# Hybrid layer: three-pass projections between the steps of the delta rule, convolution by pairs of chunks, modulation columns made in three places

## What is computed

```python
mod = cond @ mod_w[layer] + mod_b[layer]             # cond = silu(c)
sh1, sc1, g1, sh2, sc2, g2 = jnp.split(mod, 6)       # 6 x 1024
h = rmsnorm(x, norm_mix) * (1 + sc1) + sh1
qkv_a, z_a, b_a, a_a, q_b, k_b, v_b = split(h @ w_in)   # 1536, 512, 4, 4, 3 x 512
qkv_a = silu(causal_conv(qkv_a, 4 taps))             # then l2norm of q_a, k_a
o_a = rmsnorm(gated_delta_rule(q_a, k_a, v_a, g, beta)) * silu(z_a)
o_b = attention(rope(q_b), rope(k_b), v_b)           # 4 heads of 128
x = x + g1 * (concat(o_a, o_b) @ w_out)
x = x + g2 * peer_ffn(rmsnorm(x) * (1 + sc2) + sh2)  # 16384 experts, top 16
```

## Time and profile before

| | |
|---|---|
| median of 3 runs | 3955.04 us |
| the profiled execution's own time | 3955.51 us |
| its span (first to last instruction) | 3953.7 us |
| mean granted TensorE clock | 0.941 |
| TensorE busy | 3589.6 us (91%) |
| VectorE busy | 1980.6 us (50%) |
| ScalarE busy | 1753.2 us (44%) |
| DMA queue 1 | 562 MB, 43.1% of 16 engines |
| hybrid layer, start to its last product | 0 to 456.5 us |

### The profile page before, as it was taken

One profiled execution on the slowest core, in us unless ns is written; L12 is line 12 of the kernel. 1 busy time (PEld: TensorE's weight loads), 2 busy tenths in 40 slices (PEclk: granted clock), 3 DMA queues, 4 the chain that ended last, 5 costly groups with the idle time before them and its releaser, 6 DMA issues.

```text
span 3953.7 us, 54864 instructions
## 1 busy us (share of the span) xinstructions
PE 3589.6 (91%) x22798; PEld 3178.6 (80%) x22798; DVE 1980.6 (50%) x3117; ACT 1753.2 (44%) x2671; POOL 639.0 (16%) x260
## 2 busy tenths in 40 slices
PE   7777799999999889999999997979879989898799
PEld 4456699998888757999988885869879967688699
DVE  0321267565776331956655555564444446644443
ACT  1321145665444321556654543544545335345453
POOL 0000068664000000886620000000000000000000
PEclk9887899999999979999999997989899989899999
DMA  5421245445887422454456553223424623133245
GB/s 200 149 85 48 80 140 181 145 140 173 277 278 234 154 75 101 155 173 142 140 182 194 194 173 121 87 93 118 160 97 143 171 80 110 64 139 129 106 150 139
DMA packets 265628, 565.50 MB, mean 143 GB/s; under 512 B 14943, under 2 KB 91043, under 8 KB 264611
## 3 DMA queue, kind: packets, MB, share of 16 engines
q1 hardware_dynamic: 265380, 561.99, 43.1%
HBM read 560.89 MB, written 1.05 MB: 142 GB/s over the span
## 4 chain that ended last, share of the span: by engine, by line
PE 78%; DVE 6%; ACT 5%; issue 3%; DMA 2%; POOL 1%; DVEq 0%; ACTq 0%; SPq 0%
PE ps L359 7%; PE ps L361 7%; PE ps L360 7%; PE ps L286 7%; PE ps L1518 6%; PE ps L1438 6%; PE ps L1519 6%; PE ps L1439 6%; PE ps L1520 6%; PE ps L1440 6%; PE ps L1485 3%; POOL uvr_split L1809 1%; DVE ring_split L430 1%; PE ps L2122 1%; PE ps L1957 1%
## 5 line engine op out<-in xcount | busy, mean ns | idle before, releaser
L1809 POOL TENSOR_TENSOR uvr_split<-uvr,high_split 128x1024 fp32r<-128x1024 f32 x172 | 434.4, 2529 | 1301.6 <-ACT high_split L1561 1301.6
L1440 PE MATMUL ps<-consts_sb_split,uvr_split 128*128 128x256 f32 x2048 | 579.1, 283 | 0.0
L1561 ACT ACTIVATE high_split<-uvr 128x1024 fp32r<-128x1024 f32 x342 | 360.9, 1056 | 242.1 <-PE ps L1520 200.0
L361 PE MATMUL ps<-uvr_split,ring_split 128*128 128x256 f32 (+1 forms) x1584 | 454.2, 287 | 0.0
L473 ACT ACTIVATE big<-ps 128x512 f32<-128x512 f32 (+1 forms) x232 | 136.1, 586 | 627.9 <-PE ps L286 227.0
L1438 PE MATMUL ps<-consts_sb_split,high_split 128*128 128x256 f32 x1376 | 397.6, 289 | 2.9 <-ACT big L473 1.8
L1519 PE MATMUL ps<-uvr_split,hot_split 128*128 128x512 f32 x1024 | 399.1, 390 | 0.0
L1440 PEld LDWEIGHTS ps<-consts_sb_split,uvr_split 128*128 128x128 f32 x2048 | 392.0, 191 | 0.0
L1439 PE MATMUL ps<-ht_split,high_split 128*128 128x256 f32 x1376 | 389.0, 283 | 0.0
L430 DVE TENSOR_TENSOR ring_split<-big,hot_split 128x2048 fp32r<-128x2048 f32 x87 | 196.8, 2262 | 261.0 <-ACT hot_split L422 260.6
L430 DVE TENSOR_TENSOR ring_split<-big,high_split 128x2048 fp32r<-128x2048 f32 (+1 forms) x87 | 196.8, 2262 | 260.8 <-ACT high_split L422 260.3
(11 more groups left out here) (394 smaller groups left out, 8471.0 us busy)
## 6 DMA issues: line engine op xcount, KB each, us to landing
uvr<-peer_uv SPq DMA_DIRECT2D x512, 512.0 KB, 3.8
big<-mlp_w SPq DMA_DIRECT2D x32, 2048.0 KB, 8.9
big<-w_in SPq DMA_DIRECT2D x26, 2048.0 KB, 7.8
big<-mod_w SPq DMA_DIRECT2D x12, 2048.0 KB, 8.1
uvr<-mod_w SPq DMA_DIRECT2D x48, 512.0 KB, 6.6
big<-peer_w_q SPq DMA_DIRECT2D x8, 2048.0 KB, 7.9
big<-hy_w_in SPq DMA_DIRECT2D x7, 2048.0 KB, 8.7
big<-w_out SPq DMA_DIRECT2D x4, 2048.0 KB, 7.8
```

The lines of the kernel that those rows point to most:

```text
L361: m = mm(out, wl, x_high[:, k, :], start=False, stop=en)
L1440: return mm(out, w_low, x_high, start=False, stop=stop, **kw)
L1561: SE.activation(expert_high(e), expert(e), ACT.Copy).then_inc(S["expert_high"], 1)
L1809: GE.tensor_tensor(expert_low(j), expert(j), expert_high(j).bitcast(F32), ALU.subtract)\
```

## The change

- The projections of the layer become three-pass (`hybrid_linears`, a generator of 15 pieces: q/k 4, b/a 1, v 2, z 2, attention q, k, v 2 each). `hybrid_pe` runs seven at once, and the others one at a time: after the gate rows, after k.q, in each of the 5 rounds between the squaring and the inverse product, and the last behind u and w. The output projection (4 pieces) is three-pass too. The input is split in place after the block norm.
- `split_high` and `split_low` of these pieces are put between the other work of `hybrid_act` and `hybrid_dve`. The convolution runs pair by pair as the pieces come: ScalarE evicts a pair and writes the fourth tap with a scaled copy, VectorE adds three taps (36 instructions in all), ScalarE then does Silu and Square of the pair.
- Modulation tiles 0 to 3 are made on VectorE before the block norm (`mod_early_dve`: 8 scaled sums of 128x512 for each tile, then 4 small matmuls). Tiles 4 to 7 are made on TensorE behind the four chunk steps, 8 and 9 between the first heads of the attention. Tiles 10 and 11 (g2) become a seventh segment in expert layer 0.
- Rope angles and rotations move into the rounds and ahead of the chunk steps; attention follows the delta rule at once.
- `roots_act` does all Ln first, then one Exp, for every caller (the second model has callers with 6 and 4 groups; the delta rule 8 and 4).
- SP issues the vectors first, then the first modulation tile, then the other five inputs. The squares of the block norm no longer wait for the modulation.
- N (`kk_out`) is made ahead of the scaled k; the scratch places are laid out anew.

```diff
         def plan_hybrid():
-            plan_cols("gdn_qkv", w, 0, 1536)
+            plan_cols("gdn_qk", w, 0, 1024)
+            plan("gdn_ba", ...)
+            plan_cols("gdn_v", w, 1024, 1536)
             plan_cols("gdn_z", w, 1536, 2048)
-            plan("gdn_ba", ...)
-            plan_mod(0, 4, 12)
             plan_cols("moba_q", w, 2056, 2568)
             plan_cols("moba_k", w, 2568, 3080)
             plan_cols("moba_v", w, 3080, 3592)
+            plan_mod(0, 4, 10)
             plan_cols("hy_out", a["hy_w_out"][0], 0, D)

         def roots_act(rs, ngroups, mean):
...
                 SE.activation(rs[:, g0:g0 + n, :], t..., ACT.Ln, scale=1.0 / mean, bias=eps_col)
-                SE.activation(rs[:, g0:g0 + n, :], rs[:, g0:g0 + n, :], ACT.Exp, scale=-0.5)
+            SE.activation(rs[:, 0:ngroups, :], rs[:, 0:ngroups, :], ACT.Exp, scale=-0.5)

+        def mod_early_dve():
...
+            for i in range(EARLY):
+                VE.wait_ge(S[f"weights_in_{i % RING}"], weights_in(i))
+                for k in range(DC):
...
+                        VE.scalar_tensor_tensor(out=mod_total[i % 2], in0=w[:, k, :],
+                            scalar=condv[:, k:k + 1], in1=mod_total[i % 2], op0=ALU.mult, op1=ALU.add)
+                if i >= 1:
+                    columns(i - 1)

         def hybrid_pe():
             block_norm_pe(z.sq)
-            fm_linear("gdn_qkv", ...); fm_linear("gdn_z", ...); tm_linear("gdn_ba", ...)
-            mod_pe(0, 4, 8)
+            mod_early_pe()
+            linear(7)
             norm_pe([[c] for c in range(8)], 8, C["ones"], z.sq)
...
+            linear()
             TE.wait_ge(S["qk_normed"], S.nth(TE, "qk_normed"))
...
-            mod_pe(0, 8, 12)
+            linear()
             TE.wait_ge(S["n_ready"], S.nth(TE, "n_ready"))
...
-                TE.wait_ge(S["powers"], expected["powers"])
+                squared = expected["powers"]
+                linear()
+                TE.wait_ge(S["powers"], squared)
                 TE.wait_ge(S["inverse"], S.nth(TE, "inverse"))
...
+            rotate_pe("att_in", z.aq, 4, C["rot128"])
+            rotate_pe("att_in", z.ak, 4, C["rot128"])
...
+            for _ in run:
+                pass
             for c in range(NCH):
...
+                mod_unit_pe(4 + c)
             norm_pe([[c] for c in range(4)], 4, C["ones"], z.sq)
-            TE.wait_ge(S["delta_through"], S.nth(TE, "delta_through"))
-            fm_linear("moba_q", ...); fm_linear("moba_k", ...); tm_linear("moba_v", ...)
-            rotate_pe(...); rotate_pe(...)
...
+            attention_pe(4, scores, values, z.p, z.pt, between)      # mod 8, 9 at heads 0, 1
+            split_linear("hy_out", z.h_high, h_low, DC, D, "dve", "residual_in", first="x_split")

         # ScalarE, for each pair of q/k/v chunks
+            def qkv_in(i):
+                SE.activation(z.pad[:, 2 * i:2 * i + 2, 4:260], t, ACT.Copy)
+                for u in range(2):
+                    SE.activation(z.conv[:, 2 * i + u, :], t[:, u, :], ACT.Copy, scale=w[:, 2 * i + u, 3:4])
+            def silu_pair(i):
+                SE.wait_ge(S["conv_done"], S.nth(SE, "conv_done"))
...
         # expert layer 0
-        NMOD = 6 * DC
+        NMOD = 7 * DC
```

More of the change, by code:

```diff
@@ L554, in residual_dve, with gated_bank @@
             for b in range(nbanks):
[L555 to L564, removed]
-            x_complete(name)
+                gated_bank(b, gate)
+            x_complete(name)
+        def gated_bank(b, gate):
+            t = take("dve")
+            for u in range(2):
+                c = 2 * b + u
+                last = "residual_in" if u else "dve_step"
+                VE.scalar_tensor_tensor(out=x[:, c, :], in0=t[:, u * T:(u + 1) * T], scalar=gate[:, c:c + 1],
+                    in1=x[:, c, :], op0=ALU.mult, op1=ALU.add).then_inc(S[last], 1)
+                VE.wait_ge(S[last], S.nth(VE, last))
         def residual_bank(b):
@@ L1069, in hybrid_act @@
+            silu_pair(0)
+            for i in range(2, 4):
+                qkv_in(i)
+                split_high()
+                silu_pair(i - 1)
+            split_high()
+            silu_pair(3)
             SE.wait_ge(S["ba_ready"], S.nth(SE, "ba_ready"))
@@ L1075, in hybrid_act @@
             SE.wait_ge(S["ba_ln"], S.nth(SE, "ba_ln"))
+            for i in range(4, 6):
+                qkv_in(i)
+                split_high()
+            for i in range(4, 6):
+                silu_pair(i)
+            roots_act(z.rs, 8, 1.0)
+            evict_act(pairs(z.z)[0:1], ACT.Silu, frees="projections")
+            split_high()
             SE.wait_ge(S["decay_rows"], S.nth(SE, "decay_rows"))
@@ L1117, in hybrid_dve @@
+            split_low()
+            split_x_dve(h, h_low, z.h_high)
+            split_low()
             w = V["gdn_conv"].rearrange("p (c j) -> p c j", j=4)
[L1118 to L1126 removed]
@@ L1133, in hybrid_dve @@
+            for i in range(2):
+                split_low()
+                conv_pair(i)
+            split_low()
+            conv_pair(2)
+            split_low()
+            conv_pair(3)
+            VE.tensor_copy(z.ba, take("dve")[:, 0:16].rearrange("p (m n) -> p m n", m=TM)).then_inc(S["ba_out"], 1)
+            VE.wait_ge(S["ba_out"], S.nth(VE, "ba_out"))
             VE.tensor_copy(z.bb[:, :, 0:4], z.ba[:, :, 0:4]).then_inc(S["dve_step"], 1)
@@ L1775, in peer_sp @@
             uv = a["peer_uv"][L].rearrange("j p n -> p j n")
-            mod = a["mod_w"][1].rearrange("(c p) n -> p c n", p=P)
+            mod = [a["mod_w"][k].rearrange("(c p) n -> p c n", p=P) for k in range(2)]
             SP.wait_ge(S["expert_ring_free"], S.nth(SP, "expert_ring_free"))
```

406 lines of the change are left out of this document (250 added, 156 removed).

## The result

| | before | after |
|---|---|---|
| median (lowest to highest), us | 3954.3 (3948.6 to 3955.4), 4 runs | 3817.8 (3816.3 to 3821.3), 4 runs |
| profiled span, granted clock | 3953.7, 0.941 | 3816.5, 0.949 |

The ratio is 0.9657, with a 95% interval of 0.9642 to 0.9673: faster by 136.5 us. Forecast were 3818 and a range of 3788 to 3872. The sum came out to a fraction of a us.

The account below looks back on a forecast made before the run. TensorE, holding 78% of the chain's 3953.7 us, was taken as the bound. From 3955.5, minus 124.5 for the hybrid layer, plus 1.9 for g2's segment, minus 15.2 for the roots, came 3818 us; range 3788 to 3872.

Parts of the forecast that it names:

- Part 1: Start of the hybrid layer: first full-rate three-pass product near 52 us, a gain of 13 us.
- Part 2: Seven projection pieces run at once: six at 5.9 us and b/a at 5, ending near 92 us.
- Part 3: Gates to the first squaring: serial stretch with 6 us added for low clock, first squaring at 136 us against 240.5.
- Part 4: Five rounds of the inverse: 12.35 us four times and 9.7, total 59; with rotations, u and w, end at 208.5.
- Part 5: Chunk steps with modulation units, 58 us (bounds 52 and 67), ending at 266.5; then gate norm, ending at 277.
- Part 6: Attention 32 us, ending at 309; output 23 us against 29.4, ending the layer at 332 against 456.5.
- part 7: Outside the layer: +1.9 us for g2's segment, -15.2 us for fewer table loads and Exp in two layers.
- C: Rival on norms: the new Ln and Exp order spares no load, second model gives 2 us, 3831 us; chance 0.02.
- A: Rival on chunk steps: the clock stays low, 99 us for four steps instead of 58, 3859 us; chance 0.13.
- B: Rival on weight splits: they come late, exposing 4.8 us at each of twelve pieces, 3876 us; chance 0.11.
- D: Rival on TensorE: 1.2 GHz throughout the layer, added work doubles, +179 us, 3997 us; chance 0.03.
- E: Rival on the whole: nothing gained, TensorE's hours return as waits for peer weights or experts; chance 0.02.

Follow-up runs that it names:

- The run with halves: Each modulation tile of the chunk steps in two halves, eight products ahead of the wait for v, added to the run that it builds on: 3801.9 us, ratio 0.9615.
- the run that it builds on: Changed kernel with modulation tile 4 between the k.k and k.q products and the output's splits in the late order: 3807.0 us, ratio 0.9627.
- the kernel with the pairs back: Changed kernel with every norm again taking Ln and Exp pair by pair: 3853.7 us, ratio 0.9749.
- the two runs on the order: Changed kernel with Ln and Exp pair by pair again, 3853.7 us; kernel before with only all Ln first and one Exp, 3920.5 us.
- the run with the units in front: Changed kernel with modulation tiles 4 to 7 in one block ahead of the first chunk step: 3826.9 us, ratio 0.9677.
- the load order: Changed kernel with x loaded behind the second modulation tile and the constants behind the third: 3823.0 us, ratio 0.9660.
- the unit in the hole: Changed kernel with modulation tile 4 between the k.k and k.q products, the others moved up one place: 3812.5 us, ratio 0.9641.
- the late splits: Output input's first half split behind the third scores, second behind the last head, then the weight's second piece; with the unit in the hole, 3807.0 us, ratio 0.9627.
- the new start: The run with halves, plus loads as tiles 0, 1, constants, x, tiles 2, 3 and two tiles' column sums before the norm: 3795.3 us, ratio 0.9596.

## Why the prediction was right, and where it was not

The forecast case held in the main: the pieces do keep pace and hide between the steps, the modulation lies in the chunk steps, and the norms lose loads. The total is right to a us by luck, since two errors of 12 and 13 us cancelled. Of the signs that were named, the first product, the round and the wait of the query norm came as said; the end of the seven pieces, the first squaring, the layer's end and the chunk steps did not (13 to 15 us at over 0.9 were forecast, and 12.7, 17.0, 17.0 and 16.1 at 0.84 came).

**The layer gained 112.4 us, not 124.5.** By the prediction's own marks: first three-pass product 53.3 (52 forecast), seventh piece's end 100.6 (92), first squaring 142.7 (136), end of the rounds 202.6 (195), chunk steps from 215.5 (208.5) to 278.2 (266.5), gate norm 287.9 (277), first output product 318.3 (309), end 344.1 (332).

- Part 1 was off by 1.3 us. The price of 0.7 us for a sum of 512 was 0.78 (seven in 5.48 us); the arrivals 11 and 24 were 9.4 and 23.8.
- **Part 2** was off by 7.3: 47.3 us instead of 40. The pitch was right (5.9, though the prediction's own terms add up to 5.7), the clock was not. The first piece took 8.0 us, b/a 7.8 instead of 5, and the two pieces behind it 13.8 instead of 11.8. I had a clock slack in part 3 and none here, though the stretch begins behind 9 us of idle time and has narrow products in its middle.
- Part 3: 42.1 us instead of 44. My sum and its slack held, although the roots' terms, two loads, four Ln and the Exp, add up to 7.3 us and not to the 5.7 that I gave them from 100 to 105.7; they took 7.4. The largest wait, 6.5 us ahead of the last k.q products for VectorE, is that of the decays in my list: VectorE waits 5.1 us of it for ScalarE's last decay.
- Part 4: rounds of 12.2 us, 12.35 forecast, but 13.9 for the first, whose squaring took 5.47 instead of 3.74; 59.9 in all, where 59 were forecast. Rotations, u and w with the last piece took 12.8 (202.6 to 215.35) instead of 13.5.
- **Part 5**: 62.7 us instead of 58, between my bounds of 52 and 67. I chose the fast end because TensorE would be over 90% busy. It was 95% busy, and the clock fell all the same in three of the four steps, within the inner products behind a unit. The Trainium skill (TensorE: Matmul & The Clock Gate, HAM oscillation) describes bursts that start cold because of the long wait ahead of each. This trace shows a milder form: the waits are 0.85 us, the inner products start at the full clock and lose it on the way, 0.76 and 0.83 for those stretches against 0.53 before. What brings the clock down there is not shown: in the first step the same wait and the same short products ran at the full clock. The run with halves shows the price, 52.5 us for the four steps against 66.9 in the run that it builds on.
- Part 6: gate norm 9.7 us instead of 10.5, attention 30.4 instead of 32, output 25.8 instead of 23, again the low clock of its first 6 us (0.52).

**The second model gained 28 us, not 15.2.** Between before and after, the distance grew from 109.1 us at the first mixers of the second model to 137.2 at the end. The mis-sized term is part 7, the roots: 27.7 us by the loads and the Exp saved, where the sum has 15.2. I counted 2.8 us for each of two norms of four groups and 2 of 5.4 for the six groups, 7.6 us a layer, and did not count the key norm of the cross attention at all. The runs put it otherwise: 20 loads of 1.283 us are 25.7 us, the fewer Exp 2.0 more, and in the trace of the kernel with the pairs back 24 to 26 of the 28 are gone. In its stages the six groups cost some 5 us a layer, the mixers' norm 3.3 and the cross attention's two norms 4.1, 12.4 in sum. The 3.60 us of the earlier trace rows were a fair cap for the mixers' norm. Most of the error is the caution on the six groups (5 us where 2 were counted); the norm left out adds about 1, since the query norm's own wait fell by 3.07 of the 4.1. Why 2 to 4 of the 28 us stay when the pairs are back is open.

Between the two lies g2's segment, for which I added 1.9 us: the distance shrank by 3.3 (112.4 to 109.1). Two traces of like code drift by as much, so that term is neither confirmed nor refuted.

The rivals: C is refuted by the two runs on the order (36 and 33 us for 28 loads). The sentence of the Trainium skill (ScalarE: Activation LUTs, Table sets) that one set holds both ln and exp does not agree with this trace: every change between them has a row of 1.28 us. A came in part: the units took 8.6 to 9.6 us and not 14, and a clock of 0.50 throughout was seen only in the run with the units in front. B did not come: in the whole layer TensorE waited once for a split of a weight, 0.2 us in the seven pieces. D and E did not come either: the granted clock over the layer was 0.87, and the time that the layer gave is still there at the end.

## What to carry to other kernels

Count table loads in the groups of ScalarE, multiply by the duration of one, and sort the functions by table before anything else: here that alone gave a quarter of the gain. When ballast is laid into a chain, look at every wait that is left, also those under 1 us: by the traces two halves in two holes were worth 2 to 4 us a step more than the whole in one, although only some 5 us of it are sure in the kernel's time. And before a load is moved, read what stands ahead of its reader in each engine's list; the load order made the start 5.6 us longer alone, and 1.3 us shorter together with TensorE's order.

The best version measured has the unit in the hole, the halves, the late splits and the new start: 3795.3 us, ratio 0.9596 [0.9580, 0.9612] to the kernel before, 24 us below the changed kernel by the ratios.

## What the runs showed of the hardware

- In the b/a piece, 48 products of 8 columns issued without a gap, the granted clock was 0.68 with TensorE busy all of 7.8 us: it fell within them, near 81.8 us. The wide products behind, 0.28 us at full clock, took 0.41 until near 92 us. At full clock the narrow products start 0.11 us apart and those of 256 columns 0.12, so the narrow piece is hardly cheaper.
- A clock that has fallen takes the next work with it: a modulation row of 7.03 us took 8.6 to 9.6 behind the inner products, and sixteen products of the inverse 3.2 to 3.7 us instead of 1.95 behind a wait of 2.65.
- Nearly all of the time that ScalarE saved came back as time of the kernel (33 and 36 of 38.5 us), although ScalarE is busy only 46% of the span.
